# Stick-breaking attention as a running product, woven into the next head pair's panels; input norm applied at eviction

## What is computed

```python
u = x @ w_in + b_in
q, k, v, z_att, glu_a, glu_b, z_conv, g_att, g_conv = split(u)
# per head (8 heads of 64):
z = q @ k.T * 64 ** -0.5
log_fail = where(s < t, log_sigmoid(-z), 0)
later = reversed_cumsum(log_fail over s) - log_fail
w = where(s < t, exp(log_sigmoid(z) + later), 0)
att = w @ v
att_branch = (att * silu(z_att)) @ w_att_proj
c = depthwise_conv31(glu_a * sigmoid(glu_b)) + conv_b
conv_branch = (silu(layer_norm(c)) * silu(z_conv)) @ w_conv_proj + b
merged = sigmoid(g_att) * att_branch + sigmoid(g_conv) * conv_branch
out = layer_norm(ALPHA * x + merged @ w_out)
```

## Time and profile before

| what | value |
|---|---|
| median of 3 runs | 3559.89 us (3557.28 to 3561.08) |
| the profiled execution's own time | 3559.95 us |
| its span in the profile | 3558.2 us |
| mean granted TensorE clock | 0.987 of full |
| PE busy | 3449.0 us, 97% |
| DVE busy | 1464.0 us, 41% |
| ACT busy | 757.8 us, 21% |
| POOL busy | 1485.6 us, 42% |

### The profile page before, as it was taken

One profiled execution on the slowest core, in us unless ns is written; L12 is line 12 of the kernel. 1 busy time (PEld: TensorE's weight loads), 2 busy tenths in 40 slices (PEclk: granted clock), 3 DMA queues, 4 the chain that ended last, 5 costly groups with the idle time before them and its releaser, 6 DMA issues.

```text
span 3558.2 us, 38678 instructions
## 1 busy us (share of the span) xinstructions
PE 3449.0 (97%) x15180; PEld 2632.7 (74%) x15180; DVE 1464.0 (41%) x2218; ACT 757.8 (21%) x1500; POOL 1485.6 (42%) x1445
## 2 busy tenths in 40 slices
PE   7999999999999999999999999999798999999996
PEld 5777788888888787677888888878687333678875
DVE  5545541212124655546312121244459444564134
ACT  3222320102022312223202010222100454202012
POOL 5532444444444464324444444444356111355441
PEclk9999999999999999999999999999999899999998
DMA  4112121111111221121311111111111000011111
GB/s 138 46 39 72 42 59 48 49 52 48 55 48 49 79 68 43 36 80 45 54 48 48 48 55 52 50 49 45 36 48 42 6 1 1 18 45 48 48 51 66
DMA packets 341749, 173.72 MB, mean 49 GB/s; under 512 B 58048, under 2 KB 334528, under 8 KB 341568
## 3 DMA queue, kind: packets, MB, share of 16 engines
q1 hardware_dynamic: 324592, 162.49, 16.1%
q10 hardware_dynamic: 16976, 8.76, 0.8%
HBM read 155.15 MB, written 12.91 MB: 47 GB/s over the span
## 4 chain that ended last, share of the span: by engine, by line
PE 90%; DVE 8%; ACT 1%; issue 1%; ACTq 0%; DMA 0%; POOL 0%; DVEq 0%
PE ring L836 26%; PE ring L838 25%; PE ring L837 25%; DVE conv_out L1799 4%; PE ring L1104 2%; PE ring L1113 2%; PE aux L1129 2%; PE ring L1117 1%; PE aux L935 1%; PE aux L911 1%; PE aux L921 1%; PE ring L891 0%; PE ring L897 0%; PE aux L1162 0%; DVE y_out L1959 0%
## 5 line engine op out<-in xcount | busy, mean ns | idle before, releaser
L693 POOL TENSOR_TENSOR w_hi<-w_raw,ones 128x512 fp32r<-128x512 f32 (+3 forms) x568 | 620.9, 1093 | 1586.5 <-PE ring L838 1582.0
L836 PE MATMUL ring<-P_hi,w_hi 128*128 128x512 f32 x2368 | 947.4, 400 | 24.4 <-DVE P_lo L1763 14.1
L838 PE MATMUL ring<-P_hi,w_lo 128*128 128x512 f32 x2368 | 925.1, 391 | 0.0
L837 PE MATMUL ring<-P_lo,w_hi 128*128 128x512 f32 x2368 | 925.0, 391 | 0.0
L695 POOL TENSOR_TENSOR w_lo<-w_raw,w_hi 128x512 fp32r<-128x512 f32 (+3 forms) x568 | 734.2, 1293 | 44.5
L836 PEld LDWEIGHTS ring<-P_hi,w_hi 128*128 128x128 f32 x2368 | 446.0, 188 | 146.4 <-issue 45.0
L838 PEld LDWEIGHTS ring<-P_hi,w_lo 128*128 128x128 f32 x2368 | 445.9, 188 | 95.3
L837 PEld LDWEIGHTS ring<-P_lo,w_hi 128*128 128x128 f32 x2368 | 446.5, 189 | 91.1 <-issue 3.4
L836 PE MATMUL ring<-Q_hi,w_hi 128*128 128x512 f32 x1280 | 501.1, 391 | 0.0
L838 PE MATMUL ring<-Q_hi,w_lo 128*128 128x512 f32 x1280 | 498.8, 390 | 0.0
L837 PE MATMUL ring<-Q_lo,w_hi 128*128 128x512 f32 x1280 | 498.7, 390 | 0.0
(11 more groups left out here) (243 smaller groups left out, 3633.1 us busy)
## 6 DMA issues: line engine op xcount, KB each, us to landing
w_raw<-in_w_in SPq DMA_DIRECT2D x84, 512.0 KB, 3.8
w_raw<-in_w_up SPq DMA_DIRECT2D x64, 512.0 KB, 4.0
w_raw<-in_w_down SPq DMA_DIRECT2D x64, 512.0 KB, 4.0
h_scratch<-h ACTq DMA_DIRECT2D x16, 512.0 KB, 2.9
w_raw<-in_w_gate SPq DMA_DIRECT2D x16, 512.0 KB, 3.9
hx<-h_scratch SPq DMA_DIRECT2D x12, 512.0 KB, 6.7
x_raw<-in_x SPq DMA_DIRECT2D x8, 512.0 KB, 8.0
w_raw<-in_w_out SPq DMA_DIRECT2D x16, 256.0 KB, 2.7
```

The costliest lines, as they stand in the source:

```text
L693: g.tensor_tensor(w_hi[:, slot, ks], w_raw[:, slot, ks], one.broadcast_to([P, width, P]), ALU.mult).then_inc(w_hi_ready, 1)
L836: t.matmul(o, wh, xh, start=first, stop=False)
L837: t.matmul(o, wh, xl, start=False, stop=False)
L838: return t.matmul(o, wl, xh, start=False, stop=last)
```

## The change

The second block's first 24 panels become half panels as in the first block, with a table `WEAVE2`.

1. The first 8 panels read h times `final_norm` as `P_hi`, `P_lo`, which are made in the last GATE panels of the first block; DVE multiplies by rstd at eviction. Beside them DVE and ACT make the normalised x into `Q_hi`, `Q_lo` (`normalise`, `XN_PAIRS`) for all later panels. The reciprocal is in two halves.
2. The q, k, v panels are ordered by head pair c. While the panels of the next pair run, PE puts in 19 `stick` steps, one after each 2.5 chunks: at step u it makes the score of unit u (64 units in all: head, block of 128 queries; queries on the partitions, all keys up to the block, reversed), the transposes of the weights of unit u-2, and after each fourth unit the products with v (`meet`).
3. Per unit ACT makes sigmoid(-z) and sigmoid(z), DVE one `tensor_tensor_scan` (running product), POOL the product of the two, PE transposes it, ACT copies it to `weight_t`. Exp, Ln, the cap, the maximum, the running sums and the two sum matmuls are gone. The mask is one fp32r matmul of 128 columns that adds -BIG.
4. `convolve` is spread: one instruction after each stick step and each eviction, three after each for the first pair. POOL's weight splits are cut into parts that follow stick steps 1 and 3 of each panel. z_att uses Sigmoid and one multiply in place of Silu.

```diff
+def weave2():
...
+    put(1, 1, "stat", 0)
+    put(3, 1, "stat", 1)
+    for c in range(PAIRS):
+        m0 = 2 * QKV + 6 * (c + 1)
+        put(m0, 0, "turn_v2", c, 0)
+        put(m0, 1, "turn_v2", c, 1)
+        for u in range(STEPS2):
+            k = 2 + 5 * u // 2
+            put(m0 + k // 8, k % 8, "stick", c, u)
...
+        def split_part(n, part):
...
+            g.tensor_tensor(w_hi[:, slot, ks], w_raw[:, slot, ks], one.broadcast_to([P, width, P]), ALU.mult).then_inc(w_hi_ready, 1)
...
+        def weigh(unit):
...
+            pool.wait_ge(z_beta, unit + 1)
+            pool.wait_ge(z_scanned, unit + 1)
+            g.tensor_tensor(weight[:, buf, 0:n], weight[:, buf, 0:n], left[:, buf, 0:n], ALU.mult).then_inc(z_weighed, 1)
...
+        def meet(c, u):
...
+            for kb in range(7, 3 - 4 * hf, -1):
+                at = max(0, 7 - kb - 4 * hf) * P
+                mm = t.matmul(meet_bank[rows, at:HALF], v2[c % 2][:, kb, rows], weight_t[:, kb, at:HALF],
+                              start=(kb == 7), stop=True, skip_group_check=True)
...
+        def turn_weights(c, u):
...
+            pe.wait_ge(z_weighed, unit + 1)
...
+                    mm = t.transpose(turn_banks[at % 2][:, (i - first) * P:(i - first) * P + P], weight[:, unit % 2, i * P:i * P + P], ident[:])
...
+        def score(c, u):
...
+            if unit:
+                pe.wait_ge(z_beta, unit)
...
+                mm = t.matmul(score_bank[:, at:stop], query, k2[buf][rows, S - n + at:S - n + stop], start=True, stop=True)
+                if at == 0:
+                    mm = t.matmul(score_bank[:, 0:P], ident_r[:], keep_r[:], start=False, stop=True, skip_group_check=True)
...
+                    if u >= MEET_LAG and (u - MEET_LAG) % 4 == 3:
+                        meet(c, u - MEET_LAG)
+                    if TURN_LAG <= u < UNITS2 + TURN_LAG:
+                        turn_weights(c, u - TURN_LAG)
+                    if u < UNITS2:
+                        score(c, u)
...
+        def half2(m, hf):
+            no, slot = half2_no(m, hf), m % 2
+            pe.wait_ge(half_free, no - 2)
...
+            a.activation(fail[:, unit % 2, 0:n], score_bank[:, 0:n], ACT.Sigmoid, scale=-1.0).then_inc(z_failed, 1)
+            a.activation(weight[:, unit % 2, 0:n], score_bank[:, 0:n], ACT.Sigmoid).then_inc(z_beta, 1)
...
+        def take_glu(f, hf):
...
+            v.tensor_tensor(conv_in[:, f, cols], bank[no % 3], rstd[:, cols], ALU.mult).then_inc(half_free, 1)
...
+            v.tensor_tensor_scan(left[:, unit % 2, 1:n], factor, factor, 1.0, ALU.mult, ALU.min).then_inc(z_scanned, 1)
...
+        for m in range(QKV, G_ATT):
+            for hf in range(2):
+                for _, job in WEAVE2.get(2 * m + hf, ()):
+                    if job[0] == "stick":
+                        if job[2] < UNITS2:
+                            scan(*job[1:])
+                        convolve(1)
+                if m < Z_ATT:
+                    c, i = divmod(m - QKV, 3)
+                    take_qkv(c, i, hf)
+                    convolve(1 if c else 3)
+                else:
+                    take_z(m - Z_ATT, hf)
+                    convolve(1)
```

More of the change, by code:

```diff
@@ L170, with half2_no, put, rounds_before @@
 SMALL = 9
[L171 to L177, removed]
+PAIRS = 4
+def half2_no(m, hf):
+    return DEPTH * HALVES + (2 * hf + m if m < 2 else 2 * m + hf)
+UNITS2, TURN_LAG, MEET_LAG = 16, 2, 3
+STEPS2 = UNITS2 + MEET_LAG
+def weave2():
+    at = {}
+    def put(m, k, *job):
+        at.setdefault(m, []).append((k, job))
+    put(1, 1, "stat", 0)
[7 more added lines that the diff above has]
+            put(m0 + k // 8, k % 8, "stick", c, u)
+    return at
+WEAVE2 = weave2()
+XN_PAIRS = [((0, 0), (1, 0)), ((2, 0), (3, 0)), ((0, 1), (1, 1)), ((2, 1), (3, 1)),
+            ((4, 0), (5, 0)), ((6, 0), (7, 0)), ((4, 1), (5, 1)), ((6, 1), (7, 1))]
+XN_AT = {c: i for i, c in enumerate(c for pair in XN_PAIRS for c in pair)}
+def rounds_before(unit):
+    c, u = divmod(unit, UNITS2)
+    e, qb = divmod(u, 8)
+    return 24 * c + 12 * e + (qb if qb < 4 else 4 + 2 * (qb - 4))
 def in_pattern(x, g):
@@ L346, in two_blocks @@
     squares = bank[4:6]
+    score_bank, turn_banks, meet_bank = aux[0], (bank[6], bank[3]), bank[7]
     x_banks = bank[6:8]
@@ L1053, in panel2 @@
+        for i in range(4):
+            half2(*panel_of(i))
+        for m in range(2, G_ATT):
+            for hf in range(2):
+                half2(m, hf)
+        def panel2(m, src_hi, src_lo, ready, kc=KC):
+            slot, nth = m % 2, m - G_ATT
             pe.wait_ge(w_ready, 2 * (ALL + m) + 1)
[L1054 to L1058, removed]
+            if nth >= 2:
+                pe.wait_ge(slot_free, nth - 1)
+            elif nth == 0:
+                pe.wait_ge(half_free, half2_no(G_ATT - 1, 1) + 1)
@@ L1067, in panel2 @@
             mm.then_inc(panel_done, 1)
[L1069 to L1072, removed]
-        for m in range(QKV):
-            panel2(m, P_hi, P_lo, XN)
-        def turn_v2(i):
-            pe.wait_ge(slot_free, QKV + 8 + i + 1)
-            if i >= 1:
-                pe.wait_ge(v2_taken, i)
-            for j in range(8):
-                mm = t.transpose(aux[0][:, j * P:j * P + P], v2_feat[:, j * P:j * P + P], ident[:])
-            mm.then_inc(v2_turned, 1)
@@ new lines, in take_turned @@
+        def take_turned(c, u):
+            unit, qb = UNITS2 * c + u, u % 8
+            at_query = qb % 4 * P
+            for first in range(0, qb + 1, 4):
+                at, n = rounds_before(unit) + first // 4, min(4, qb + 1 - first)
+                kb = 7 - qb + first
+                act.wait_ge(z_turned, at + 1)
+                a.activation(weight_t[:, kb:kb + n, at_query:at_query + P], turn_banks[at % 2][:, 0:n * P].rearrange("p (b q) -> p b q", b=n), ACT.Copy)\
+                    .then_inc(z_taken, 1)
@@ L1410, in branch_high @@
[L1410 to L1416 removed]
+        def branch_high(f):
+            act.wait_ge(branched, f + 1)
+            a.activation(branch_hi[:, f], conv_out[:, f], ACT.Copy).then_inc(hi2_ready, 1)
@@ new lines, in _ @@
+        dve.wait_ge(gains_loaded, 16 * 8)
+        dve.wait_ge(small_loaded, 16 * SMALL)
+        for hf in range(2):
+            invert(DEPTH, 0, hf)
+            normalise(2 * hf)
+            take_glu(0, hf)
+            take_glu_gate(0, hf)
+            normalise(2 * hf + 1)
+        for f in range(1, 4):
+            for i in range(4):
+                if 4 * f + i <= 7:
+                    normalise(4 * f + i)
+                if i < 2:
+                    take_glu(f, i)
+                else:
+                    take_glu_gate(f, i - 2)
```

506 lines of the change are left out of this document (267 added, 239 removed).

## The result

The changed kernel takes 3505.8 us (3498.4 to 3506.1, 4 runs) against 3558.6 (3556.1 to 3561.1, 4 runs): 0.9847 of the time, interval 0.983 to 0.9864. That is 53 us less where 102 less were forecast. The profiled execution took 3505.59 us, 54.4 less than that of before.

A forecast was written before the change was run, and what follows sets the result against it. PE was taken as the bound, busy for 97% of the span. Attention -82, front -39, branch -5 and waits in the weave +24 gave -102: 3559.95 - 102 = 3458 us, range 3432 to 3500.

The forecast's parts named there:

- The attention work on PE, -82: Second block's attention matmuls and transposes on PE: 210 us against 291.5, so -82 us (-86 to -48).
- the sum without waits: Whole kernel if PE never waits in the weave: 3429 us, given as 3429 to 3434 before the experiments.
- The front, -39: Second block's start and q, k, v panels: 46 us of standing still and low clock go, 2 and 5 come.
- the branch, -5: Before G_ATT: 5.75 us of wait and about 1 at low clock go, about 1.6 us of wait comes.
- Where PE will wait in the weave: PE's waits among woven attention steps: 12 us at eight largest units, 12 us at others, +24 us.
- all other units: Units besides the eight largest: a convolution or weight split can stand in front, 12 us more of waits.
- waits this short cost no clock: PE's waits in the weave: after one of 1.17 us the transposes and panel behind ran at full speed.
- DVE becomes the bound: Rival in the weave: scan costs like the reciprocal, DVE 45 to 49 us a head, 3505 to 3525 us; chance 0.10.
- DVE and POOL take turns: Rival in the weave: DVE and POOL instructions with SBUF inputs cannot overlap, 3480 to 3505 us; chance 0.14.

The follow-up runs named there:

- Kernel 9: Changed kernel with the product on DVE, an elementwise product for the scan and only the convolution's first tap: 3433.8 us, 0.9651.
- Kernel 1: Changed kernel with POOL's weight splits after the second and fourth attention step of a panel instead of the first and third: 3479.9 us, 0.9784.
- Kernel 3: Changed kernel with an elementwise product of the same inputs in place of the scan, running product left out: 3467.0 us, 0.9748.
- kernel 5: Changed kernel with one more wait on DVE, so the convolution after a scan waits for POOL's product of that unit: 3512.0 us, 0.9877.
- kernel 2: Changed kernel without the convolution's 120 accumulating DVE instructions, only the first tap kept: 3465.1 us, 0.9743.
- kernel 11: Changed kernel with the product on DVE, the later weight splits and the uneven attention steps together: 3446.8 us, 0.9689.
- kernel 7: Changed kernel with the unit's product on DVE right behind the scan, POOL keeping only the weight splits: 3456.4 us, 0.9715.
- Kernel 10: Changed kernel with attention steps at uneven chunks instead of every 2.5, more room before the long units' transposes: 3474.6 us, 0.9759.
- kernels 6: Changed kernel with both the later weight splits and DVE's convolution waiting for POOL's product: 3501.5 us, 0.9842.
- kernel 8: Changed kernel with the product on DVE and weight splits after the second and fourth attention step: 3455.0 us, 0.9709.

## Why the prediction was right in kind and wrong in size

**The attention work on PE, -82: right.** Kernel 9 measures it: 213.2 us for attention, turns of v and sums of squares where the sum had 216, and 3433.8 us as a whole where the sum without waits had 3429 to 3434. Transposes cost what the earlier trace rows said, four in 0.43 to 0.53 us in kernel 9. The mask was too cheap in my list at 0.13 us: it takes 0.17 before a panel matmul and 0.26 before a second piece of the score, which is half of the units each, so 5 to 6 us more over 64 of them. Something else, which I haven't found, was some 8 us too dear.

**The front, -39, and the branch, -5: right.** GLU follows the gate panels without a gap at 2499.6, and PE waits once, for 3.28 us at 2532.09, 32.5 us behind the start, where I had 4 and 1 and the eviction at 32. The branch's two losses became one of 1.66 us. With what lies behind G_ATT the branch gave 5.8 us: 7.45 less from G_ATT's first panel to the end, and the 1.66 before it.

**"Where PE will wait in the weave", +24: wrong, and the step that failed.** The place was right: eight waits of over 1 us, one for each head's largest unit, for POOL's product, and nearly nothing for evictions. The size was 46 us of waits (the sum had 22 too few) and 26 us beyond the sum's matmul prices that are in no wait (none in the sum); together 72 for 24, which is the whole error of 48. Kernel 9 shows that they are lower clock, and puts it at 29, since it finds the matmuls 3 us cheaper than the sum had them. The waits came about in three ways.
- I gave splits and convolutions ahead of a product 12 us over "all other units", where 6.0 of waits came, and none at the largest, where a split stands every time: 38.5 us for the 12 that I had there. I counted POOL's queue as a load and did not walk it in program order. Kernel 1 gives that 26 us.
- The scan was priced like an elementwise product, 1.4 us. It is 2.28 undisturbed for 1023 columns, beside 1.31 for the elementwise product of the same inputs (kernel 9), 1.7 times as much. Kernel 3 gives 39 us for the difference, since PE stands still 22 us less and is busy 13 us less for the same matmuls.
- DVE and POOL lengthen each other's work. I had 1.5 us in each of eight units for all of this; a product of 128 columns has 1376 ns where it has 459 (kernel 5) to 514 (kernel 2) with no convolution beside it, and the chain of the largest unit, sigmoid and hand-overs set aside, ran 8.9 us where scan and product have 2.3 + 2.3.

The claim "waits this short cost no clock" rested on one wait of 1.17 us. Behind one of 1.45 here the panel ran at the lower level (2649.15), and so it did behind the waits of 4 to 5.6 us, though not behind those of 1.37 and 1.75. Kernel 9 shows the size, kernel 11 (clock in the weave 0.98) that it shrinks when the waits do. What besides the wait decides whether the clock falls stays open.

**The rivals.** The time came out at the lower end of "DVE becomes the bound", whose mechanism was not there: the scan has no reciprocal's price (2.3 us, not 6.6), and in kernel 7 DVE is busy for 321 of 388 us instead of 304 of 436, with less waiting of PE. Nor does that rival's range follow from its own terms: 40 to 75 and 16 us on the 3434 that the sum has without waits in the weave give 3490 to 3525, and on 3458 they give 3514 to 3549. It came out just above "DVE and POOL take turns", whose mechanism was there: in kernel 5's timeline each of the two waits for the end of the other's instruction and then does its own work, within 0.2 us. But I had worked that rival out as two full queues at equal load to PE. What it did was to lengthen the latency of one chain; POOL was busy for 247 of the 436 us.

**Open.** Kernel 11 is still 13 us above kernel 9. Its waits for ACT are 8.4 us; issuing ACT's gate and branch copies elsewhere wasn't tried. How the shares of split, turns and scan add up can't be said from single removals, since each removal took part of the same waits. Kernel 10 has one run at 3465.7 us beside others near 3475, which nothing here explains. Which matmul price in the attention sum was too dear isn't known either.

## What to carry to other kernels

Where a chain of several engines must close before PE comes back, walk each engine's queue in program order up to the one instruction that matters, above all for the longest unit: what is queued in front of it counted whole (a split, 26 us here), though POOL was busy for only 247 of 436 us. Two links with SBUF inputs, one on VectorE and one on GpSimd, were better put on the faster of the two (1.23 us for the product of 1024 keys against 2.34), one behind the other, even though it was the busier (49 us here); an added wait that keeps the engines apart only moved the loss (not faster, 6 us more in the median). And waits on PE are to be priced with the clock that may fall with them: here 46 us of waits brought 26 to 29 more, but how much depends on more than their length.

## What the runs showed of the hardware

- **The scan.** 2.28 us for 1023 f32 columns and 1.22 for 511, undisturbed (kernels 6 and 8), about 2.1 ns a column: 1.7 to 1.9 times an elementwise product (1.31 for the same inputs in kernel 9, 1.23 for the unit's product of 1024).
- **VectorE and GpSimd.** An f32 product of two SBUF inputs on GpSimd takes 459 ns for 128 columns and 2338 for 1024 when VectorE is quiet (kernel 5); beside convolutions 1376 and 2812. A scan beside a split took 3.36 us instead of 2.28. In kernel 5's timeline the loser's time is the rest of the other's instruction and then its own, within 0.2 us. VectorE's evictions of q, k and v out of PSUM (512 columns, with a bias) kept their 0.74 us (0.736 to 0.751 in all 24 of the changed kernel), also in the middle of a GpSimd product (2742.56).
- **The clock.** Behind a wait of 1.45 us amid other attention steps, the next panel matmuls ran at the lower of the two levels (granted clock 0.50 instead of 1.00, 0.43 us a matmul instead of 0.23), and after 5.63 us they did so for 4.3 us; waits of 1.75 and, in kernel 10, of 2.21 to 2.27 us were followed by no fall. Over the weave the granted clock was 0.92 with 46 us of waits (after the change), 0.98 with 19 (kernel 7), 0.96 with 13 (kernel 8), 0.98 with some 8 (kernel 11) and 1.00 with some 2 (kernel 9).
- **The mask matmul** (fp32r, 128 columns) took 0.17 us from start to start before a panel matmul and 0.26 before an f32 score, both at full clock.
- **Hand-overs**, 0.1 us each in my list: 0.04 us from the end of ACT's sigmoid to the scan (2660.14 to 2660.18, kernel 7), 0.15 from the scan to GpSimd's product (2666.67 to 2666.82, kernel 5), 0.05 from VectorE's product to the transposes (2662.66 to 2662.71, kernel 8).
- **Writing in place** on GpSimd cost nothing here: 1376 ns either way, beside convolutions.
